# Grouped attention: query heads paired across key heads, two key panels in place of four

## The reference, cut to what matters

```
def gqa_project(h, w_qkv, q_norm, k_norm):
    qkv = h @ w_qkv
    q = qkv[..., :nq].reshape(b, t, GQA_KV_HEADS, GQA_GROUP, GQA_HEAD_DIM).transpose(0, 2, 3, 1, 4)
    k = qkv[..., nq:nq + nk].reshape(b, t, GQA_KV_HEADS, GQA_HEAD_DIM).transpose(0, 2, 1, 3)
    v = qkv[..., nq + nk:].reshape(b, t, GQA_KV_HEADS, GQA_HEAD_DIM).transpose(0, 2, 1, 3)
    return rms_norm(q, q_norm), rms_norm(k, k_norm), v

def gqa_mixer(hl, hc, w_qkv, q_norm, k_norm, w_o, tables, with_ctx):
    ...
    ql = apply_axial_rope(ql, tables)
    kl = apply_axial_rope(kl, tables)
    k_all = jnp.concatenate([kc, kl], axis=2)
    v_all = jnp.concatenate([vc, vl], axis=2)
    ol = merge_heads(blocked_attend(ql, k_all, v_all)) @ w_o
```

## Time and profile before

| | us |
|---|---|
| median of 3 runs | 2370.72 |
| lowest and highest run | 2370.48, 2375.87 |
| span of the profiled execution | 2366.9 |
| PE busy in the span | 2234.1 (94%) |
| DVE busy | 1513.2 (64%) |
| ACT busy | 949.3 (40%) |
| POOL busy | 47.3 (2%) |

### The profile page before, as it was taken

The page is one execution under the profiler, slowest core; times in us unless marked ns, Lnnn a source line. Parts: engine busy times, 40 slices in busy tenths (PEclk is TensorE's granted clock), DMA queues, the critical chain, the costliest instruction groups (busy, mean ns, idle before and its releaser), DMA issues.

```text
span 2366.9 us, 39554 instructions
## 1 busy us (share of the span) xinstructions
PE 2234.1 (94%) x15920; PEld 1958.1 (83%) x15920; DVE 1513.2 (64%) x2394; ACT 949.3 (40%) x1504; POOL 47.3 (2%) x43
## 2 busy tenths in 40 slices
PE   6999899999999989999999978899999999899998
PEld 3655678888767689999999867799989999688997
DVE  4789663544456765676667874576676675756666
ACT  3224532222234744453354343444353452345433
POOL 0000000000004000000002000000000000000000
PEclk9999999999999999999999999999999998999999
DMA  7778223222222045555554302345545543233553
GB/s 287 264 256 301 78 74 98 90 97 91 88 89 81 19 169 183 180 169 185 180 168 156 121 29 65 123 153 182 181 145 185 183 146 130 67 134 116 187 186 116
DMA packets 93990, 340.48 MB, mean 144 GB/s; under 512 B 10272, under 2 KB 12448, under 8 KB 93600
## 3 DMA queue, kind: packets, MB, share of 16 engines
q1 hardware_dynamic: 92528, 333.42, 41.9%
q10 hardware_dynamic: 1328, 5.21, 0.6%
HBM read 337.54 MB, written 1.05 MB: 143 GB/s over the span
## 4 chain that ended last, share of the span: by engine, by line
PE 87%; DVE 7%; ACT 3%; DMA 2%; issue 1%; SPq 0%; DVEq 0%; ACTq 0%
PE ps L536 22%; PE ps L538 21%; PE ps L537 21%; PE ps L941 2%; PE ps L641 2%; DMA ring<-weights 2%; PE ps L548 1%; PE ps L549 1%; PE ps L559 1%; PE ps L1213 1%; DVE WS L2035 1%; PE ps L711 1%; PE ps L1035 1%; DVE RS L2443 1%; PE ps L890 1%
## 5 line engine op out<-in xcount | busy, mean ns | idle before, releaser
L2035 DVE TENSOR_TENSOR WS<-ring,WS 128x1024 fp32r<-128x1024 f32 x487 | 599.0, 1233 | 393.8 <-ACT WS L1488 392.3
L1488 ACT CAST WS<-ring 128x1024 fp32r<-128x1024 f32 x487 | 507.3, 1044 | 613.0 <-PE ps L538 512.6
L536 PE MATMUL ps<-HS,WS 128*128 128x256 f32 x1968 | 561.7, 285 | 2.5 <-DVE WS L2035 2.5
L538 PE MATMUL ps<-HS,WS 128*128 128x256 f32 x1968 | 558.6, 284 | 0.0
L537 PE MATMUL ps<-HS,WS 128*128 128x256 f32 x1928 | 547.4, 284 | 0.0
L536 PEld LDWEIGHTS ps<-HS,WS 128*128 128x128 f32 x1968 | 379.4, 193 | 4.8 <-DVE WS L2035 3.7
L538 PEld LDWEIGHTS ps<-HS,WS 128*128 128x128 f32 x1968 | 379.2, 193 | 0.0
L537 PEld LDWEIGHTS ps<-HS,WS 128*128 128x128 f32 x1928 | 371.7, 193 | 1.0 <-issue 1.0
L536 PE MATMUL ps<-HTS,WS 128*128 128x256 f32 x960 | 272.7, 284 | 2.4 <-DVE HTS L2115 1.6
L537 PE MATMUL ps<-HTS,WS 128*128 128x256 f32 x960 | 272.0, 283 | 0.0
L538 PE MATMUL ps<-HTS,WS 128*128 128x256 f32 x960 | 271.9, 283 | 0.0
(11 more groups left out here) (418 smaller groups left out, 3207.1 us busy)
## 6 DMA issues: line engine op xcount, KB each, us to landing
ring<-weights SPq DMA_DIRECT2D x633, 512.0 KB, 3.4
X<-xs ACTq DMA_DIRECT2D x1, 2048.0 KB, 9.2
con<-const ACTq DMA_DIRECT2D x1, 2016.0 KB, 10.1
X<-mem ACTq DMA_DIRECT2D x1, 1024.0 KB, 5.6
y<-X SPq DMA_DIRECT2D x4, 256.0 KB, 2.2
vecs<-vec SPq DMA_DIRECT2D x1, 311.5 KB, 7.9
con<-const SPq DMA_DIRECT2D x1, 130.0 KB, 9.0
```

The source lines that it names most:

```text
L536: pe.matmul(dst, w[0][:, cut], upper, start=first, stop=False, skip_group_check=True)
L538: return pe.matmul(dst, w[1][:, cut], upper, start=False, stop=last, skip_group_check=True)
L1488: act.copy(WS[:, split % HALVES, 0, :], ring[:, panel % RING, :]).then_inc(uppers_ready, 1)
L2035: dve.tensor_tensor(WS[:, split % HALVES, 1, :], ring[:, panel % RING, :], WS[:, split % HALVES, 0, :].bitcast(F32), ALU.subtract).then_in ...
```

## The change

Two different key heads share a panel (256 key columns as two panels of 128), and a query tile holds two heads that use two different key heads: tile j = 4n + i holds query heads 8n + i (key head 2n, partitions 0 to 63) and 8n + 4 + i (key head 2n + 1, partitions 64 to 127). The query columns and the rows of `w_o` are put in that order on the host. The stage has 12 panels and 6 tiles to rotate.

```diff
+def head_columns():
+
+    heads = [8 * n + 4 * x + i for n in range(2) for i in range(4) for x in range(2)]
+    return np.concatenate([np.arange(64 * h, 64 * h + 64) for h in heads])
...
-    keys = qkv[:, 1024:1280].reshape(D, 4, 1, 64)
-    add(k_panels(np.concatenate([keys, keys], 2).reshape(D, 512)))
-    add(k_panels(qkv[:, :1024]), qkv[:, 1280:1536].reshape(2, 4, P, 256).transpose(0, 2, 1, 3).reshape(2, P, D))
-    add(k_panels(a["gqa_w_o"][0]))
+    add(k_panels(qkv[:, 1024:1280]))
+    add(k_panels(qkv[:, head_columns()]), qkv[:, 1280:1536].reshape(2, 4, P, 256).transpose(0, 2, 1, 3).reshape(2, P, D))
+    add(k_panels(a["gqa_w_o"][0][head_columns()]))
...
-        KQ_BANK = (0, 1, 4, 5, 0, 1, 4, 5)
-        GQA_PANELS = 14
+        KQ_BANK = (0, 1, 4, 5, 0, 1)
+        KEYS, UNITS = 2, 6
+        GQA_PANELS = 12
...
             def queries(u):
 
-                pe.wait_ge(act_done, at("act", f"kq_raw{u - 4}"))
+                if u >= 4:
+                    pe.wait_ge(act_done, at("act", f"kq_raw{u - 4}"))
                 for q in range(2):
                     split_tile(ps[:, KQ_BANK[u], q * T:(q + 1) * T], f"kq{u}", q == 0, lambda half, k: CH[:, half, k, LAT])
+                    if u == KEYS and q == 0:
+                        key_sum(0)
+                        key_sum(1)
...
-            split_tile(ps[:, KQ_BANK[2], :], "kq2", True, conv_halves)
-            key_sum(0)
-            key_sum(1)
-            split_tile(ps[:, KQ_BANK[3], :], "kq3", True, conv_halves)
-            key_sum(2)
+            queries(2)
+            queries(3)
+            query_sums(2)
             kq_rotated(0)
             queries(4)
-            key_sum(3)
+            query_sums(3)
             kq_rotated(1)
             queries(5)
             query_sums(4)
             kq_rotated(2)
-            queries(6)
+            pe.wait_ge(act_done, at("act", "kq_raw3"))
+            value_rows(0)
             query_sums(5)
             kq_rotated(3)
             kq_rotated(4)
-            queries(7)
-            query_sums(6)
+            value_rows(1)
             kq_rotated(5)
-            pe.wait_ge(act_done, at("act", "kq_raw5"))
-            value_rows(0)
-            query_sums(7)
-            kq_rotated(6)
-            value_rows(1)
-            kq_rotated(7)
-            pe.wait_ge(act_done, at("act", "kq_rms3"))
+            pe.wait_ge(act_done, at("act", "kq_rms1"))
...
-                            ins = pe.matmul(ps[:, 2 * (p % 2) + x, :], KQ[rows, 4 + j // 2, at_q:at_q + P], KQ[rows, j // 2, :],
+                            ins = pe.matmul(ps[:, 2 * (p % 2) + x, :], KQ[rows, KEYS + j // 2, at_q:at_q + P], KQ[rows, j // 4, :],
...
+                                head = 2 * (j // 4) + x
-                                                GV[:, l, (j // 2) * 64:(j // 2 + 1) * 64], PT2[:, w % 2, x, l * P:(l + 1) * P],
+                                                GV[:, l, head * 64:(head + 1) * 64], PT2[:, w % 2, x, l * P:(l + 1) * P],
...
             lowers("gqa", 3, 5)
             key_norm(0)
-            lower("gqa", 5)
+            lowers("gqa", 5, 7)
             key_norm(1)
-            lower("gqa", 6)
+            lower("gqa", 7)
             kq_rotated(0)
-            lower("gqa", 7)
-            key_norm(2)
             lower("gqa", 8)
             kq_rotated(1)
-            lower("gqa", 9)
-            key_norm(3)
-            lower("gqa", 10)
+            lowers("gqa", 9, 11)
             kq_rotated(2)
```

More of the change, by code:

```diff
@@ L768, in key_sum @@
                 pe.wait_ge(act_done, at("act", f"kq_sq{u}"))
-                pe.wait_ge(act_done, at("act", "n2rms" if u < 2 else f"kq_rms{u - 2}"))
+                pe.wait_ge(act_done, at("act", "n2rms"))
                 s.step(pe.matmul(ps[:, 2 + u % 2, :], blk, SQ[:, u % 2, :], start=True, stop=True).then_inc(pe_done, 1), f"kq_sum{u}")
@@ L774, in query_sums @@
                 pe.wait_ge(act_done, at("act", f"kq_sq{u}"))
-                pe.wait_ge(act_done, at("act", "kq_rms2"))
+                pe.wait_ge(act_done, at("act", "kq_rms0"))
                 pick = blk.rearrange("p (x c) -> p x c", x=2)[:, :, 0]
                 for n in range(4):
-                    p = 4 * (u - 4) + n
+                    p = 4 * (u - KEYS) + n
                     ins = pe.matmul(ps[:, 2, 2 * p:2 * p + 2], SQ[:, u % 2, n * P:(n + 1) * P], pick, start=(p == 0), stop=True,
@@ L783, in kq_rotated @@
             def kq_rotated(w):
-                pe.wait_ge(*(after("dve", f"kq_norm{w}") if w < 4 else after("act", f"kq_raw{w}")))
+                pe.wait_ge(*(after("dve", f"kq_norm{w}") if w < KEYS else after("act", f"kq_raw{w}")))
                 if w >= 2:
@@ L802, in value_rows @@
                         x = [CH[:, half, k, t * P:(t + 1) * P] for half in range(2)]
[L803 removed]
+                        dst = ps[:, 4 + t // 2, (t % 2) * T:(t % 2 + 1) * T]
                         pe.matmul(dst, x[0], w[0][:, cut], start=(k == 0 and t % 2 == 0), stop=False, skip_group_check=True)
@@ L883, in paired_attention @@
                         if p % 4 == 0:
-                            pe.wait_ge(pool_done, at("pool", f"kq_cos{4 + j // 2}"))
+                            pe.wait_ge(pool_done, at("pool", f"kq_cos{KEYS + j // 2}"))
                         if p >= 2:
@@ L1683, in _ @@
             act.dma_start(MEMN, mem).then_inc(inputs_in[3], 16)
-            for u in range(8):
-                if u >= 4:
-                    upper("gqa", 2 * u - 1)
+            for u in range(UNITS):
+                if u >= KEYS:
+                    upper("gqa", 2 * u + 1)
                 act.wait_ge(splits_used, at("split", f"kq{u}"))
@@ L1691, in _ @@
                 s.step(act.activation(SQ[:, u % 2, :], got, ACT.Square).then_inc(act_done, 1), f"kq_sq{u}")
[L1692 to L1696, removed]
+                s.step(act.activation(KQ[:, u, :], got, ACT.Identity, scale=v("gqa_q") if u >= KEYS else 1.0).then_inc(act_done, 1), f"kq_raw{u}")
+                if u == 1:
+                    uppers("gqa", 3, 5)
+                    kq_rms(0)
+                    kq_rms(1)
+                if KEYS <= u < UNITS - 1:
+                    upper("gqa", 2 * u + 2)
                 if u == 3:
                     act.wait_ge(inputs_in[3], 16)
-                if 4 <= u < 7:
-                    mem_squares(2 * u - 8, 2 * u - 6)
+                if 3 <= u < UNITS:
+                    mem_squares(2 * u - 6, 2 * u - 4)
             mem_squares(6, 8)
-            act.wait_ge(pe_done, at("pe", "kq_sum7"))
+            act.wait_ge(pe_done, at("pe", "kq_sum5"))
             s.step(act.activation(QR, ps[:, 2, 0:32], ACT.Sqrt, bias=eps6, scale=1.0 / 64).then_inc(act_done, 1), "q_rms")
@@ L1705, in _ @@
             for q in range(2):
-                s.step(act.copy(GV[:, 2 * q:2 * q + 2, :], ps[:, q, :].rearrange("p (t c) -> p t c", t=2)).then_inc(act_done, 1), "gv")
+                s.step(act.copy(GV[:, 2 * q:2 * q + 2, :], ps[:, 4 + q, :].rearrange("p (t c) -> p t c", t=2)).then_inc(act_done, 1), "gv")
             act.wait_ge(pe_done, at("pe", "memsum"))
@@ L2315, in kq_rotated @@
                 for half in range(2):
-                    sin = c("gqa_sin")[:, half * T:(half + 1) * T] if w < 4 else c("gqa_sin")[:, T:2 * T]
+                    sin = c("gqa_sin")[:, half * T:(half + 1) * T] if w < KEYS else c("gqa_sin")[:, T:2 * T]
                     ins = dve.tensor_tensor(ROT[:, w % 2, half * T:(half + 1) * T], ps[:, 6 + w % 2, half * T:(half + 1) * T],
@@ L2345, in _ @@
             s.step(dve.tensor_scalar(QN, QR, -64 ** -0.5, None, ALU.mult).then_inc(dve_done, 1), "q_scale")
-            kq_rotated(7)
+            kq_rotated(5)
             def attention(tag, units, scale, out_src, out_dst):
@@ L2845, in _ @@
             pool.wait_ge(inputs_in[4], 16)
-            for u in range(8):
+            for u in range(UNITS):
                 pool.wait_ge(pe_done, at("pe", f"kq_rot{u}"))
                 for half in range(2):
-                    cos = c("gqa_cos")[:, half * T:(half + 1) * T] if u < 4 else c("gqa_cos")[:, T:2 * T]
+                    cos = c("gqa_cos")[:, half * T:(half + 1) * T] if u < KEYS else c("gqa_cos")[:, T:2 * T]
                     q = KQ[:, u, half * T:(half + 1) * T]
```

7 lines of the change are left out of this document (1 added, 6 removed).

## The result

| | before | after |
|---|---|---|
| median of the runs | 2373.30 us (4 runs, 2370.48 to 2378.33) | 2360.56 us (4 runs, 2359.07 to 2361.20) |
| ratio, with 95% interval | | 0.9944 [0.9930, 0.9959] |
| profiled execution: span | 2366.9 us | 2357.2 us |
| granted clock, mean over the span | 0.980 | 0.975 |

The kernel is faster by 0.56%. The forecast was 2356.9 in a range of 2353.1 to 2361.6: the time fell inside, 3.7 us above it. The profiled spans differ by 9.7 us, though the changed stage alone gave 13.8. Where the other 4 went is most of what follows. In this experiment and all that follow, an execution's time lies 1.8 to 2.2 us above its own span. So the 3.8 us between the median of three runs and the span of 2366.9, in the text ahead, say that the profiled execution of the kernel before was one of its faster ones.

A forecast was written before the change was run, and what follows sets the result against it. PE's own queue was taken to bound the stage. 14.62 us of removed work less 0.79 of waits gave 13.8; the span of 2366.9 became 2353.1, plus 3.8 gave 2356.9 us, range 2353.1 to 2361.6.

The forecast's parts named there:

- The work taken off PE: In the changed stage, 48 matmuls of 128x512 (11.20 us) and four plain float32 ones (3.42) leave PE's queue: 14.62 us.
- The new waits: In the changed stage, PE waits for late conversions at panel 3 (0.13 us) and panel 5 (0.66): 0.79, ends 0 and 2.5.
- POOL's overlap: POOL's cosine products slow conversions 7 and 9 by up to 0.7 us each, some 0.3 seen at panel 9.
- The stage: Key and query panels up to the sums of squares: 14.62 us of PE work less 0.79 of waits gives 13.8.
- The rival of a half-clock attention: Clock falls at the attention's start, 46.19 us of PE work become 92, total 2403 us; slower had chance 0.02.
- the pace of the conversions as a bound: Panels 3, 5, 7 and 9 each come about 1 us late: gain 10 to 11, some 2360 us; chance 0.15.
- the half gain: Matmuls cheaper than their spacing, or another bound behind the stage: half of 14.6 us goes, about 2363; chance 0.05.
- that the change does not do what it says: Rival that PE's work isn't less; held closed but for the waits, as panels and matmuls are gone; no separate chance.
- the same length from there to the end: From the attention's start to the program's end the order and length stay as before, so the 13.8 us carries over.
- stretches behind it stood longer at half clock: Sign of being wrong, behind the attention; half-clock stretches were given 3 us each way in the range.
- The base: Starting time of the whole program: profiled span 2366.9 us, with the runs' median 3.8 above it.
- the first rival: Conversions set the stage's pace: 4 us lost, gain 10 to 11, some 2360 us; chance 0.15.

The follow-up runs named there:

- PE's work restored: Changed kernel with 48 matmuls of 128x512 and four plain float32 ones put back on PE, no conversions, norms or transfers: 2374.89 us, 1.0007.
- the products alone: Changed kernel with only the 48 matmuls of 128x512 of the two dropped key tiles run again, into an unused bank: 2375.17 us, 1.0007.

## Why the prediction was right, and what it missed

- **The work taken off PE** was 14.62: right. 48 matmuls measured 11.22 (11.20 predicted), four plain ones 3.43 (3.42). The Trainium skill's page "TensorE: Matmul & The Clock Gate", section "Back-to-back issue gap", would have had about 131 ns for each of the 48. The run that put them back doesn't agree: it shows 234 ns.
- **The new waits** were 0.13 and 0.65 (0.13 and 0.66 predicted), with none at panels 7 and 9. The range of 0 to 2.5 for them wasn't needed. POOL's overlap took 0.57 of the microsecond to spare at panel 7.
- **The stage** gave 13.81 (13.8 predicted). The sums of squares came at 741.85 and the attention at 746.03, 1.7 ahead of the 743.5 and 747.7 forecast; 1.6 of it is an earlier start of the stage. Of that 0.5 came ahead of the first key panel (683.76 against 684.28), and 1.1 in the first two panels, which took 12.90 in place of 13.99. Both differ from one execution to the next: two profiles of the kernel before have 12.90 too.
- **The attention** kept its 50.60 us, clock 1.00. The rival of a half-clock attention fell. So did, as mechanisms, the pace of the conversions as a bound, the half gain, and that the change does not do what it says.
- **What failed** is the step "the same length from there to the end". The recurrence, some 680 us on, stood at half clock in nearly every run of the changed kernel and in 35 of 76 runs of the other, as the mean clock has it. The prediction named "stretches behind it stood longer at half clock" as a sign of being wrong, but gave such stretches 3 us each way, as noise around a mean of 0. The mean isn't 0: one costs 5.1 us, and (23/24 - 35/76) x 5.1 is an estimated 2.5. Then -13.8 + 2.5 is -11.3; over all 14 runs of the changed kernel the mean is 2362.6, and 2373.8 - 2362.6 is 11.2, give or take 1.7.
- **The base** hid it. The profile before was of an execution without that stretch, while almost half of that kernel's have it. And the median of three runs that the forecast started from, 2370.7, is 3.1 us below the mean of the 76 later ones.
- **Luck** had a part in the number. The four runs of the result have a median of 2360.56, inside the range of 2353.1 to 2361.6. The ten further runs have 2363.51, and the mean of all 14 is 2362.6, both above it: by 3.1 for the base and 2.6 for the gain, this is 5.7 over the forecast. The gain of 11.2 is also nearer to the first rival's 10 to 11 than to the forecast's 12 to 16, though not by that rival's mechanism.

What stays open is why the changed kernel falls in nearly all of its executions. What one fall costs is shown by the profiles with and without it. That its greater share takes the 2.5 us fits the runs with the matmul that prevents it (a difference of 13.3 in place of 11.2), though each of these has its 1.7 us of doubt. The cause of the share isn't shown. The instruction count had no fair test. PE's work restored (8 of 12 runs) and the products alone (8 of 10) lie between the two kernels, too few runs to say more. The time of the recurrence within the execution and the conversions and norms that are gone remain as candidates, and weren't tried apart.

## What to carry to other kernels

Where one engine is full and its clock is whole, the time that a removed piece gives is the spacing of its instructions, less the new waits, which could be followed through the other engines' queues to a tenth of a microsecond here. It isn't always so: the same way of reasoning missed by 0.7 us where one conversion was moved ahead. Before the gain is carried to the end of the program, look for stretches behind it that hold the clock in some executions only, by the granted clock of many runs and not by one profile: here one such place, some 680 us behind the change, took about a fifth of the gain. One wide matmul that fits into a wait ahead of it, put into both kernels, brought the difference back to 13.3 of 13.8.

## What the runs showed of the hardware

- The recurrence's queue of small matmuls went to half clock with PE busy for 12.69 of 13.70 us in the fallen stretch, and in only part of the executions of one program, where it was worth 5.1 to 5.4 us in the profiles. With a single matmul of 0.86 us in a wait of 1.06 ahead of it the fall was in none of 4 profiles, and none of 30 runs had the mean clock of a fall.
- Plain float32 matmuls of 32 columns went to half clock though PE was busy for all of 8.00 us and all of 9.10 us, and cost 0.34 us each on average, against 0.86 for 512 columns at full clock. Narrow ones aren't cheap.
- PE's transposes in the attention, 128 of them among the score and value matmuls, didn't cost it the clock, neither before nor after (1.00 over 50.6 us). The Trainium skill's page "TensorE: Matmul & The Clock Gate", Part 4 ("PE-mode transpose"), states that the full clock doesn't engage for transposes. These windows don't agree for such a mix; no run has transposes alone.
